# Hybrid decoder trunk on one core: the first two weight slabs of the mixer taken in another order, and the rotation of k inside its slab

## The reference: what is computed

```
x <- LN1(alpha*x + 0.5*SwiGLU_1(x))
x <- LN2(alpha*x + W_o( sum_b g_b(x) * P_b(mixer_b(x)) ))
x <- LN3(alpha*x + 0.5*SwiGLU_2(x))

proj = x @ w_in + b_in
(aq, ak, av, mq, mk, mv, mo, mi, mf, cx, cb, cc, gates) = jnp.split(proj, _split_points(), axis=-1)
aq = partial_rope(aq.reshape(B, S, N_Q_HEADS, HEAD_DIM), positions)
ak = partial_rope(ak.reshape(B, S, N_KV_HEADS, HEAD_DIM), positions)
y_attn = sliding_window_attention(aq, ak, av, sinks)
h = mlstm_chunkwise(mq, mk, mv, mi, mf)
```

## Time and profile before

| | |
|---|---|
| median of 3 runs | 2470.65 us (2470.32 to 2471.61) |
| the profiled execution's own time | 2470.8 us |
| its span, first to last instruction | 2469.0 us |
| PE busy | 2444.2 us, 99% of the span |
| DVE, ACT busy | 1068.7 us, 766.8 us |
| mean granted clock of TensorE | 0.997 |

### The profile page before, as it was taken

How to read it: one execution, slowest core, us unless ns; L and a number is a source line. 1 busy time by engine, 2 the same in 40 slices (tenths; PEclk the granted TensorE clock), 3 DMA queues, 4 the chain that set the end, 5 groups by cost and what they waited for, 6 DMA issues and landing times.

```text
span 2469.0 us, 27519 instructions
## 1 busy us (share of the span) xinstructions
PE 2444.2 (99%) x11756; PEld 2037.1 (83%) x11756; DVE 1068.7 (43%) x1566; ACT 766.8 (31%) x1128; POOL 17.1 (1%) x16
## 2 busy tenths in 40 slices
PE   8999999999999999999999999999999999999998
PEld 7888888778888888888888888887788888888887
DVE  3333246455555553332443332554555556433324
ACT  3222123344343232221232221233444332322211
POOL 0000200000000000000000000000000000000000
PEclk9999999999999999999999999999999999999999
DMA  5332234222223323332233232342232223332232
GB/s 179 103 103 89 104 100 128 77 78 85 86 69 103 137 88 100 102 100 91 100 103 103 86 102 103 99 129 69 69 100 72 85 103 119 103 103 89 100 108 81
DMA packets 204970, 243.40 MB, mean 99 GB/s; under 512 B 10288, under 2 KB 166960, under 8 KB 204848
## 3 DMA queue, kind: packets, MB, share of 16 engines
q1 hardware_dynamic: 204848, 241.63, 29.7%
HBM read 235.31 MB, written 6.29 MB: 98 GB/s over the span
## 4 chain that ended last, share of the span: by engine, by line
PE 99%; DVE 1%; DMA 0%; ACT 0%; issue 0%; SPq 0%; DVEq 0%
PE main L1247 22%; PE main L1249 21%; PE main L1248 21%; PE main L1345 5%; PE main L1347 4%; PE main L1346 4%; PE side L1346 4%; PE side L1345 4%; PE side L1347 4%; PE main L1328 1%; PE main L1329 1%; PE main L1330 1%; PE side L1270 1%; PE side L1500 1%; PE side L1462 1%; PE side L1486 0%
## 5 line engine op out<-in xcount | busy, mean ns | idle before, releaser
L1247 PE MATMUL main<-xh,wh 128*128 128x512 f32 x2128 | 839.1, 394 | 5.8 <-DVE mvt L942 5.8
L1248 PE MATMUL main<-xh,wl 128*128 128x512 f32 x2128 | 831.0, 391 | 0.0
L1249 PE MATMUL main<-xl,wh 128*128 128x512 f32 x2128 | 830.7, 390 | 0.0
L793 DVE TENSOR_TENSOR wl<-raw,wh 128x1024 fp32r<-128x1024 f32 (+2 forms) x440 | 498.6, 1175 | 722.1 <-ACT wh L526 721.7
L526 ACT ACTIVATE wh<-raw 128x1024 fp32r<-128x1024 f32 (+2 forms) x440 | 423.7, 1012 | 703.4 <-PE main L1249 305.5
L1247 PEld LDWEIGHTS main<-xh,wh 128*128 128x128 f32 x2128 | 400.7, 188 | 96.4 <-DVE mvt L942 7.5
L1249 PEld LDWEIGHTS main<-xl,wh 128*128 128x128 f32 x2128 | 400.7, 188 | 84.8
L1248 PEld LDWEIGHTS main<-xh,wl 128*128 128x128 f32 x2128 | 401.0, 188 | 81.4 <-issue 0.5
L896 DVE SCALAR_TENSOR_TENSOR hp<-main,sil 128x512 f32<-128x512 f32 x88 | 56.7, 686 | 306.3 <-PE main L1249 297.1
L587 ACT ACTIVATE hh<-hp 128x512 fp32r<-128x512 f32 x88 | 54.1, 632 | 353.3 <-DVE hp L896 353.3
L1345 PE MATMUL main<-wh,hh 128*128 128x512 f32 x352 | 137.7, 391 | 0.0
(11 more groups left out here) (232 smaller groups left out, 2280.0 us busy)
## 6 DMA issues: line engine op xcount, KB each, us to landing
raw<-gu SPq DMA_DIRECT2D x176, 512.0 KB, 4.5
raw<-w_in SPq DMA_DIRECT2D x100, 512.0 KB, 4.6
raw<-down SPq DMA_DIRECT2D x80, 512.0 KB, 4.2
raw<-w_branch SPq DMA_DIRECT2D x24, 512.0 KB, 4.1
raw<-w_out SPq DMA_DIRECT2D x16, 512.0 KB, 4.1
raw<-w_in SPq DMA_DIRECT2D x28, 256.0 KB, 3.4
raw<-down SPq DMA_DIRECT2D x16, 256.0 KB, 2.8
spill<-xt SPq DMA_DIRECT2D x8, 512.0 KB, 6.2
```

Source lines behind the costliest of these rows:

```text
L793: ins = V.tensor_tensor(put(wl[slot]), get(raw[slot]), f32(put(wh[slot])), ALU.subtract)
L1247: T.matmul(out, hi, rh(k), start=k == 0, stop=False)
L1248: T.matmul(out, lo, rh(k), start=False, stop=False)
L1249: ins = T.matmul(out, hi, rl(k), start=False, stop=k == kk - 1)
```

## The change

Three things are moved; no operation is added or removed. In `first_rows`, PE takes token tiles 0 and 1 of slab 0, transposes tile 2, and only then takes tiles 0 and 1 of slab 1. In ACT's `norm_tail`, the root of tile 3 stands ahead of the copy of tile 2. In slab 5 of the mixer, PE's rotation of k moves from behind the slab to its middle (ahead of two small transposes), and DVE empties bank 1 (`rows_out(layer, 4)`) ahead of k's three rotation operations instead of behind them.

```diff
@@ norm_tail of ACT
                     split(g + 1)
                     split(g + 2)
-                    high(L + 1, 2)
                 root(L, 3)
                 if L < NORMS - 1:
+                    high(L + 1, 2)
                     high(L + 1, 3)
@@ mixer of DVE
                     if s == 5:
+                        rows_out(layer, NB)
                         rope(layer, 4, kT[:, :], 0)
-                        for i in range(NB, 2 * NB):
+                        for i in range(NB + 1, 2 * NB):
                             rows_out(layer, i)
@@ first_rows of PE
                 tile_of(0, 0)
+                tile_of(1, 0)
+                turn_tile(v, 2)
                 tile_of(0, 1)
-                turn_tile(v, 2)
-                tile_of(1, 0)
                 tile_of(1, 1)
                 turn_tile(v, 3)
                 for t, s in ((2, 0), (3, 0), (2, 1), (3, 1)):
@@ middle_job of PE
                 if s == 5:
+                    rotate(layer, 4, kT[:, :], 0, 4)
                     pe.wait_ge(carry.sem, carry.val(layer, 1))
@@ end_job of PE
-                if s == 5:
-                    rotate(layer, 4, kT[:, :], 0, 4)
```

## The result

The changed kernel takes 2455.76 us (median of 4 runs, 2455.45 to 2456.16), the kernel before in the same comparison 2471.13 us (2470.32 to 2473.23). The ratio is 0.9937, 95% interval 0.9919 to 0.9954: faster by 0.6%. The forecast was 2455.7 us. The profiled execution took 2455.77 us with a span of 2454.0, against 2470.8 and 2469.0.

A forecast was written before the change was run, and what follows sets the result against it. PE's own work was taken to bound the kernel (99% of the chain), so removed waits and their clock loss come back: 2 x 2.18 + 4.67 + 5.96 = 15.0 us, forecast 2455.7 us, range 2453.5 to 2461.0.

The forecast's parts named there:

- First slabs, 2.18 us per layer: In the first two slabs, PE's new tile order removes the 1.91 us wait for low weights, gaining 2.18 us per layer.
- Tile 3's margin: In the first slabs, tile 3's low part was to be ready 0.4 to 0.5 us before PE wants it.
- The rotation, 4.67 and 5.96 us: At slab 5, moving k's rotation gains 4.67 us in layer 1 and 5.96 in layer 2: 2.90 wait each, rest clock.
- DVE's margin for bank 0: At slab 5's end, DVE was to empty bank 0 at 436.8, 2.1 us before PE ends the slab.
- The order of bank 1: At slab 5, bank 1's earlier copy takes 0.4 us off DVE's way without being needed for it.
- no clock loss at all in the timed runs: Bound for both places: only waits are regained, 2 x (2.18 + 2.90) = 10.2 us, giving 2460.5 us.
- The half clock: Rival at slab 6: waits go but the slow clock stays, from another cause such as the rotation; 2460.5 us, chance 0.04.
- the banks taken in turn: Rival in the first slabs: more bank changes lower the clock, costing up to 3.06 us per layer; 2461.8 us, chance 0.04.
- no wait took the place of another: Rival: a new wait cancels one place's gain, 2460.1 us (first slabs) or 2466.3 us (slab 5); chance 0.07.
- PE's transposition of tile 2: Slower rival in the first slabs: this transposition waits for z_ready and blocks PE; 2475.5 us or more, chance 0.02.
- the first place failing: The first slabs gain nothing, so 4.4 us come back: 2460.1 us, chance 0.04.
- the second place gains nothing: Moving k's rotation at slab 5 gains nothing, so 10.6 us come back: 2466.3 us, chance 0.03.

The follow-up runs named there:

- e1: Kernel before with only the first slabs changed (PE's order of tiles and ACT's root): 2465.61 us, ratio 0.9978.
- e2: Kernel before with only PE's rotation of k and DVE's copy of bank 1 moved: 2461.60 us, ratio 0.9962.
- e4: Changed kernel with ACT's root of tile 3 put back behind the copy of tile 2: 2455.76 us.
- e7: Kernel before with only ACT's root of tile 3 moved ahead of the copy of tile 2: 2472.42 us, ratio 1.0002.
- e3: Changed kernel with DVE's copy of bank 1 put back behind k's rotation operations: 2455.79 us.
- e10: Kernel before with DVE's copies of banks 1 and 0 between k's second and third rotation operations: 2467.59 us, ratio 0.9988.
- e9: Changed kernel, rotation still in mid-slab, with DVE copying bank 0 last and slab 6 waiting for all four copies: 2465.03 us over 11 runs.
- e8: Changed kernel with DVE's low weights of the mixer's second slab put behind the last scaling and tile 2's low part: 2464.38 us.
- e5: Kernel before with only DVE's copies of banks 1 and 0 moved ahead of k's rotation operations: 2461.69 us, ratio 0.9961.
- e6: Kernel before with only DVE's copy of bank 1 moved ahead of k's rotation operations: 2468.88 us, ratio 0.9991.

## Why the prediction was right

**The bound.** PE holds the chain, so waits removed from PE come back as time. Shown by e1 and e2, each with one place changed, and by the stretches above: between the two mixers nothing moved.

**First slabs, 2.18 us per layer.** Measured 2.17 and 2.18. The order of PE does it: e4, without the root's move, has the whole gain, and e7, the root alone, none. Tile 3's margin was put at 0.4 to 0.5 us; PE did not wait, and DVE's last low part ends at 385.75 where the prediction's arithmetic, 383.99 + 12 x 0.18 + 0.1, asks for it at 386.2 (PE's first matmul of tile 3 is at 386.23): 0.5 us in hand.

**The rotation, 4.67 and 5.96 us.** The measured stretches gave 4.72 and 6.03. The rotation costs 0.86 in mid-slab rather than 0.90: from 429.59 to the second matmul behind the transposes (431.01) it is 1.42 us, and without the rotation the same work took 0.56. DVE's margin for bank 0 was 2.2 us where 2.1 were forecast.

**The order of bank 1.** Said to be off the way; e3 shows it.

**The clock, where the size was right and its place too narrow.** The prediction took the whole clock loss to be at slab 5, since the profiled execution had it there, and put the loss behind the 1.91 us waits at nothing. The profiles of e2, e7 and e10 each show one fall there too, at 1.5 to 1.6 us. This term was missing; it is why e2's median came 1.5 us above its expectation.

The total did not suffer by it. The prediction took from the profiled execution's time what this same execution had lost, and this one had lost nothing behind its 1.91 us waits. The same subtraction on e7's profile, with PE's waits as before, by the same four stretches, is 3.70 + 2.18 + 4.63 + 5.98 = 16.5 us, and 2472.63 less that is 2456.1, an estimate of the same time from an execution with a larger loss. The changed kernel's time was therefore well founded. The size of the gain, 15.4 us by the medians against 15.0, was in part luck: all runs of the kernel before, 60 of them, spread from 2469.0 to 2473.2 us with a median of 2470.6, and the one profiled, 2470.8, happened to lie near it. The Trainium skill's statement in "TensorE: Matmul & The Clock Gate" (Part 1) that the count of slow matmuls varies between runs of one kernel agrees with this case: 2469.2 to 2472.7 us at mean clocks of 0.998 to 0.996 for the kernel before in the last comparison, 2455.5 to 2456.2 at 0.999 for the changed one, whose only wait left is that of the start.

The bound "no clock loss at all in the timed runs" was not met: the lowest of all runs of the kernel before, 2469.0, is still some 3 us above 2455.8 + 4.35 + 5.8 = 2465.9. Each of its 60 runs lost something; of the 56 whose mean granted clock is known none has more than 0.998.

**The rivals.** The half clock did not stay, the banks taken in turn did not lower it (1.00 in all four windows), no wait took the place of another, and PE's transposition of tile 2 found its `z_ready` long given (375.38, wanted at 378.02).

**Two slips in the prediction's bounds.** Its range was said to reach up to the case "without any clock loss and the first place failing (2460.5)". Each of the two alone gives 2460.5 or 2460.1, but together they leave only the 5.8 us of waiting at slab 5: 2464.9. And the case "the second place gains nothing", 2466.3, lies 4.4 us from no change, within the 4.9 us that it called indistinguishable, yet was counted as faster. Neither touches the forecast.

**Left open.** What makes the clock fall behind one gap and not behind the next. The rotation right ahead is not needed for a fall (e9's profile) and does not ensure one (e10's layer 1, two runs of e1). The length of the gap alone does not decide either: 1.91 us was followed by a fall in e2, e7 and e10, and 2.86 us was not in e8. And of the kernels with waits of 2.90 us at slab 5, e1 and e9 had runs near no loss and the kernel before had none in 60. These two lack the 1.91 us waits ahead in the first slabs, which before has; whether that is the reason was not tested.

## What to carry to other kernels

Where one engine holds the chain, its list of waits, with the slower work behind each, is the whole budget for an edit that only moves work. For each wait, look in the waiting-for engine's own queue for work that stands ahead of what is wanted and isn't needed for it: here three operations ahead of two bank copies, and an order of tiles that asked for the second slab about 2 us before it could be there. Price an idle gap on TensorE as the gap plus the slower matmuls behind it, and take that second part from several executions, not from one.

## What the runs showed of the hardware that was not expected

A granted clock below 1.00 followed some of PE's idle gaps and not others, in the same kernel and for the same length of gap. All gaps in the mixers of the kept profiles, two per profile and place:

| gap, and what PE did ahead of it | profiles | gaps | clock fell | cost beyond the gap |
|---|---|---|---|---|
| 1.91 us, ordinary matmuls | before, e2, e5, e6, e7, e10 | 12 | 3 | 1.5 to 1.6 us |
| 2.05 us, rotation | e10 | 2 | 1 | 1.9 us |
| 2.56 us, rotation | e6 | 2 | 2 | 1.9 us |
| 2.86 us, transposition of a tile | e8 | 2 | 0 | none |
| 2.90 us, rotation | before, e1, e7 | 6 | 6 | 1.7 to 1.9 or 3.1 us |
| 2.90 us, ordinary matmuls | e9 | 2 | 2 | 1.9 and 3.1 us |

The 2.90 us gap of one kernel cost 1.8 us more in one layer and 3.1 in the other. Gaps can cost more than their length, and they make a kernel less repeatable: the 60 runs of the kernel before spread over 4.2 us and the 11 of e9 over 5.9, while the 14 runs of the three kernels without a wait in the mixers (the changed one, e3, e4) spread over 1.6.
